# Stick-breaking attention scored three units ahead, with its running sums multiplied as two reduced-precision parts

## The reference

```
z = q k^T * scale                                   # masked: key < query
log_1m_beta = log_sigmoid(-z)                       # = -softplus(z)
between = reverse_cumsum(log_1m_beta) - log_1m_beta # over the keys
out = exp(log_sigmoid(z) + between) v
```

## Time and profile before

| | |
|---|---|
| median of 3 runs | 1580.63 us (1580.37 to 1584.75) |
| profiled execution, its own time | 1585.6 us |
| its span in the trace | 1583.5 us |
| mean granted TensorE clock | 0.977 of full |
| busy, share of the span | PE 94%, DVE 42%, ACT 33%, POOL 19% |
| the stage `heads` with its attention units | from 530.8 us to about 762.8 us |

### The profile page before, as it was taken

How to read it: one execution, slowest core, us unless ns; L and a number is a source line. 1 busy time by engine, 2 the same in 40 slices (tenths; PEclk the granted TensorE clock), 3 DMA queues, 4 the chain that set the end, 5 groups by cost and what they waited for, 6 DMA issues and landing times.

```text
span 1583.5 us, 27315 instructions
## 1 busy us (share of the span) xinstructions
PE 1481.2 (94%) x11281; PEld 1144.9 (72%) x11281; DVE 663.1 (42%) x1053; ACT 525.4 (33%) x945; POOL 306.2 (19%) x412
## 2 busy tenths in 40 slices
PE   5989989989898898998999999999999999999997
PEld 5767777767677554554678788888888888888876
DVE  5244152555653353546274424233332424242336
ACT  4432231433322466767343402122030403021122
POOL 5574615423241241513000100000000000000000
PEclk9999989999999899999999999999999999999999
DMA  5544413423233603003242312112020202111015
GB/s 184 139 136 134 113 42 99 130 57 96 58 83 96 175 5 81 2 2 127 95 152 80 123 37 66 40 40 66 9 97 0 93 13 66 40 43 63 26 44 182
DMA packets 134937, 124.10 MB, mean 78 GB/s; under 512 B 20813, under 2 KB 112138, under 8 KB 134842
## 3 DMA queue, kind: packets, MB, share of 16 engines
q1 hardware_dynamic: 88556, 92.90, 18.9%
q10 hardware_dynamic: 46286, 29.84, 6.7%
HBM read 97.88 MB, written 24.84 MB: 77 GB/s over the span
## 4 chain that ended last, share of the span: by engine, by line
PE 46%; DVE 2%; ACT 1%; DMA 1%; issue 1%; POOLq 0%; SPq 0%; DVEq 0%; ACTq 0%
PE all_ps_b L2028 22%; PE all_ps_b L2005 21%; PE all_ps_b L1577 2%; DMA bk_acc<-in_w_out 1%; POOLq L1597 0%; DVE bk_acc L1872 0%; PE all_ps_b L1998 0%; ACT bk_acc L1766 0%; DVE bk_acc L1882 0%; DVE bk_w1L L1843 0%; DVE bk_acc L1868 0%; DVE all_hL L1888 0%; DVE all_gL L1914 0%; ACT bk_rect L1797 0%; DVE bk_acc L1955 0%
## 5 line engine op out<-in xcount | busy, mean ns | idle before, releaser
L2005 PE MATMUL all_ps_b<-all_hH,bk_w1L 128*128 128x512 f32 x512 | 200.2, 391 | 5.4 <-PE all_ps_b L2028 2.1
L1924 DVE TENSOR_TENSOR bk_acc<-bk_acc,all_ps_b 128x512 f32<-128x512 f32 x128 | 88.0, 688 | 276.0 <-PE all_ps_b L2028 275.2
L2028 PE MATMUL all_ps_b<-bk_w2H,all_gL 128*128 128x512 f32 x512 | 199.9, 390 | 2.5 <-DVE all_gL L1914 2.5
L2028 PE MATMUL all_ps_b<-bk_w2L,all_gH 128*128 128x512 f32 x512 | 199.9, 390 | 0.0
L2028 PE MATMUL all_ps_b<-bk_w2H,all_gH 128*128 128x512 f32 x512 | 199.7, 390 | 0.0
L2005 PE MATMUL all_ps_b<-all_hH,bk_w1H 128*128 128x512 f32 x512 | 199.3, 389 | 0.0
L2005 PE MATMUL all_ps_b<-all_hL,bk_w1H 128*128 128x512 f32 x512 | 199.2, 389 | 0.0
L1205 PE MATMUL fr_ps_F<-fr_hH,fr_wL 128*128 128x512 f32 (+1 forms) x416 | 175.0, 421 | 7.2 <-POOL fr_wL L457 7.2
L457 POOL TENSOR_TENSOR fr_wL<-fr_raw,fr_wH 128x256 fp32r<-128x256 f32 (+1 forms) x208 | 162.1, 811 | 32.6 <-ACT fr_wH L502 29.3
L1205 PE MATMUL fr_ps_F<-fr_hH,fr_wH 128*128 128x512 f32 (+1 forms) x416 | 165.2, 397 | 0.0
L1205 PE MATMUL fr_ps_F<-fr_hL,fr_wH 128*128 128x512 f32 (+1 forms) x416 | 165.0, 397 | 0.0
(11 more groups left out here) (343 smaller groups left out, 2238.2 us busy)
## 6 DMA issues: line engine op xcount, KB each, us to landing
fr_raw<-in_w_in ACTq DMA_DIRECT2D x37, 512.0 KB, 4.2
bk_raw<-in_w_ff SPq DMA_DIRECT2D x32, 512.0 KB, 4.2
all_raw<-in_w_ff SPq DMA_DIRECT2D x32, 512.0 KB, 4.8
projected<-fr_stage ACTq DMA_DIRECT2D x39, 256.0 KB, 4.4
fr_raw<-in_w_in SPq DMA_DIRECT2D x13, 512.0 KB, 4.3
fr_xt<-in_x SPq DMA_DIRECT2D x8, 512.0 KB, 5.5
bk_acc<-in_x SPq DMA_DIRECT2D x8, 512.0 KB, 3.3
x_after_mixers<-bk_acc SPq DMA_DIRECT2D x8, 512.0 KB, 2.7
```

The lines of the kernel that those rows point to most:

```text
L1924: dve.tensor_tensor(acc[:, j, ds], acc[:, j, ds], ybank[g % 4][:], ALU.add).then_inc(collected, 1)
L2005: m = pe.matmul(bank[s][h][:], w[s][:, k, :], a[:, k, hs], start=(k == 0 and q == 0), stop=(k == KB - 1 and q == 2))
L2028: m = pe.matmul(ybank[g % 4][:], a[:, i, ts], w[:, i, ds], start=(i == 0 and q == 0), stop=(i == FB - 1 and q == 2))
```

## The change

1. AHEAD goes from 2 to 3. On PE the order within a unit becomes sums(u), scores(u+3), values; on ACT weight(u), then exp and ln of unit u+3 next to each other (a new `logs`). PE issues the first three scores of the next pair at the end of a pair, and ACT their logs.
2. The softplus is written over E (SP = E). The wait for POOL's running sum moves from DVE's softplus to ACT's exponential.
3. POOL copies the softplus to an fp32r tile SPH (`high`), DVE subtracts it one unit later into SPL (`low`), and `sums` multiplies fp32r `tri` by both instead of float32 `tri` by SP. The matmul of `ones` by R stays float32.
4. POOL's running sum and the GLA pieces of POOL and DVE move one unit behind in their queues. DVE's `scale`, the copies of the mixed result and SPLIT_AT move later (SCALE_AT 7 to 8, SPLIT_AT 8 to 10). Two of DVE's 13 `split_low` come after the last unit.

```diff
-    NZ, AHEAD = 4, 2
+    NZ, AHEAD = 4, 3
-        SP = [r.sb(f"SP{n}", [P, HALF]) for n in range(4)]
+        SP = E
+        SPH = [r.sb(f"SPH{n}", [P, HALF], F32R) for n in range(4)]
+        SPL = [r.sb(f"SPL{n}", [P, HALF], F32R) for n in range(3)]
-        SQUARE_AT, SUM_AT, ROOT_AT, SCALE_AT = 0, (2, 4), (3, 5), 7
-        HIGH_AT, LOW_AT = SCALE_AT + 2, SCALE_AT + 4
-        SPLIT_AT = 8
+        SQUARE_AT, SUM_AT, ROOT_AT, SCALE_AT = 0, (2, 4), (3, 5), 8
+        HIGH_AT, LOW_AT = SCALE_AT + 1, SCALE_AT + 4
+        SPLIT_AT = 10
 # POOL
+                def high(u):
+                    pool.wait_ge(s("sp"), i * NU + u + 1)
+                    if u >= 4 or i:
+                        pool.wait_ge(s("tri_mm"), i * NU + u - 3)
+                    pool.tensor_copy(SPH[u % 4][:, span(u)], SP[u % 4][:, span(u)]).then_inc(s("sp_high"), 1)
+                for u in range(NU):
+                    high(u)
+                    if u:
+                        running(u - 1)
+                    gla(i * NU + u - 1)
+                running(NU - 1)
 # ACT
+            def logs(i, u):
+                act.wait_ge(s("z"), i * NU + u + 1)
+                if u >= 4 or i:
+                    act.wait_ge(s("sum"), i * NU + u - 3)
+                act.activation(E[u % 4][:, span(u)], Z[u % NZ][:, span(u)], ACT.Exp).then_inc(s("exp"), 1)
+                act.wait_ge(s("exp"), i * NU + u + 1)
+                act.activation(E[u % 4][:, span(u)], E[u % 4][:, span(u)], ACT.Ln, bias=1.0).then_inc(s("log"), 1)
 # DVE
+                def low(u):
+                    dve.wait_ge(s("sp_high"), i * NU + u + 1)
+                    if u >= 3 or i:
+                        dve.wait_ge(s("tri_mm"), i * NU + u - 2)
+                    dve.tensor_tensor(SPL[u % 3][:, span(u)], SP[u % 4][:, span(u)],
+                                      SPH[u % 4][:, span(u)].bitcast(F32), ALU.subtract).then_inc(s("sp_low"), 1)
                 for u in range(NU):
                     softplus(u)
+                    if u:
+                        low(u - 1)
...
-                    gla(i * NU + u)
+                    gla(i * NU + u - 1)
+                low(NU - 1)
+            for n in range(NU - AHEAD - SPLIT_AT, len(ahead.pieces)):
+                ahead.split_low(dve, n)
 # PE
-                    pe.wait_ge(s("sp"), i * NU + u + 1)
-                    m = pe.matmul(z, tri[:], SP[u % 4][:, span(u)], start=False, stop=True, skip_group_check=True)
+                    pe.wait_ge(s("sp_high"), i * NU + u + 1)
+                    pe.matmul(z, tri[:], SPH[u % 4][:, span(u)], start=False, stop=True, skip_group_check=True)
+                    pe.wait_ge(s("sp_low"), i * NU + u + 1)
+                    m = pe.matmul(z, tri[:], SPL[u % 3][:, span(u)], start=False, stop=True, skip_group_check=True)
```

More of the change, by code:

```diff
@@ L2613, in units, with running @@
                 nth = [0, 0]
-                for u in range(NU):
+                def high(u):
[3 more added lines that the diff above has]
+                    pool.tensor_copy(SPH[u % 4][:, span(u)], SP[u % 4][:, span(u)]).then_inc(s("sp_high"), 1)
+                def running(u):
                     h, c, kb, off, first = UNITS[u]
@@ L2674, in mixed_high, with take_values @@
                 act.copy(ahead.hH[:, i, :], outT[:]).then_inc(s("m_high"), 1)
-            def units(i):
[L2677 to L2691, removed]
+            def take_values(i, n):
+                act.wait_ge(s("v_mm"), i * 2 + n + 1)
+                act.copy(vn[:, 4 * n:4 * n + 4, :], X[:].rearrange("p (j f) -> p j f", f=P)).then_inc(s("v"), 1)
+            def logs(i, u):
[5 more added lines that the diff above has]
+                act.activation(E[u % 4][:, span(u)], E[u % 4][:, span(u)], ACT.Ln, bias=1.0).then_inc(s("log"), 1)
+            def units(i):
                 def weight(u):
@@ L2697, in weight @@
                     act.activation(W[u % 4][:, span(u)], Z[u % NZ][:, span(u)], ACT.Exp).then_inc(s("weight"), 1)
-                for u in range(-AHEAD, NU):
+                for u in range(NU):
+                    weight(u)
                     if u + AHEAD < NU:
[L2701 to L2705, removed]
-                    elif i < LAST:
-                        split(i + 1, u + AHEAD - NU)
+                        logs(i, u + AHEAD)
+                    elif i < LAST:
+                        if u < NU - 1:
+                            split(i + 1, u + AHEAD - NU)
+                        else:
+                            for n in range(AHEAD):
+                                logs(i + 1, n)
                     if i == LAST and 0 <= u - SPLIT_AT < len(ahead.pieces):
@@ L2710, in units @@
                     if u == 0:
-                        take_values(1)
+                        take_values(i, 1)
                     if u == TAKE_AT:
@@ L2721, in units @@
                         mixed_high(i - 1)
-                    if u >= 0:
-                        gla(i * NU + u)
+                    gla(i * NU + u)
                 take_output(i, 1)
+                if i < LAST:
+                    take_values(i + 1, 0)
             act.preload_act_table_set(EXP_LN)
             act.wait_ge(s("eps"), 1)
+            take_values(0, 0)
+            for n in range(AHEAD):
+                logs(0, n)
             for i in range(PAIRS):
@@ L2873, in values @@
                     m.then_inc(s("v_mul"), 1)
-                for u in range(-AHEAD, NU + 1):
+                for u in range(NU + 1):
+                    if u < NU:
+                        sums(u)
                     if u + AHEAD < NU:
-                        scores(u + AHEAD)
-                    if 0 <= u < NU:
-                        sums(u)
+                        scores(i, u + AHEAD)
+                    if u == NU - 1 and i < LAST:
+                        for n in range(AHEAD):
+                            scores(i + 1, n)
                     if u >= 2 and u % 2 == 0:
                         values(u - 2)
+                    if u == NU and i < LAST:
+                        turn_values(i + 1, 0)
                     if u == 0:
@@ L2885, in units @@
                         squares(i - 1, SUM_AT.index(u))
-                    if 0 <= u < NU:
+                    if u < NU:
                         gla(i * NU + u)
+            turn_values(0, 0)
+            for n in range(AHEAD):
+                scores(0, n)
             for i in range(PAIRS):
```

37 lines of the change are left out of this document (16 added, 21 removed).

## The result

| | median us | runs |
|---|---|---|
| before | 1580.75 | 13 |
| changed kernel | 1586.64 | 13 |

The ratio is 1.0029 (95% interval 1.0017 to 1.0041): slower by 0.3%, where 1575.0 was forecast.

What follows compares the result with a forecast made beforehand. The stage was taken as PE-bound in 86 us and bound by chains across engines in most of the rest. -4.2 + 1.6 - 2.8 - 0.8 + 0.6 = -5.6 us took 1580.63 to 1575.0; range 1561 to 1588.

Steps and rivals of the forecast that it cites:

- Ends of pairs 0 and 1, -4.2: Units 14 to 23 of pairs 0 and 1: PE's saving partly lost, -2.1 us each, bounds 0 and -7.2.
- Load permits it: Ends of pairs 0 and 1: DVE at 21.7 and 24.0 us, POOL about 17, fit within 28.3 and 27.3.
- The chain: Ends of pairs 0 and 1: sums(u-2) through softplus and subtraction to `ones`, 4.3 us plus about 0.2 for two units.
- Narrow units, -0.8: Units 0 to 13 of pairs 0 and 1, 0 to 7 of the last: together -0.8 us, bounds -7 and +8.
- The comparison behind a wait: Narrow units, way to the next weight: a wash at 512 columns, a loss of 0.1 to 0.3 at 128 and 256.
- The +3.5 for ACT's exponential behind the weight: Narrow units: ACT reaches its linear-attention piece one exponential later, some six places at 0.6, +3.5 us.
- The last pair, +1.6: Last pair: subtractions and POOL's work exclude each other, 2.72 us a unit against 2.58; +1.6 us, bounds -3.6 and +6.
- Steps, -2.8: Between pairs, last weight to first: splits one unit earlier, scores ahead; -1.4 us twice, bounds 0 and -5.
- Start, +0.6: Before the first sums: one more unit's scores and logs and one subtraction, +0.6 us.
- PE's saving: Triangular sums: two fp32r matmuls for one float32 save 0.40 us a unit at 512 columns; ceiling 21.5 us.
- the slower one: Rival: VectorE and GpSimd exclude each other on every unit's path, `low` behind POOL's addition; about 1590 us, chance 0.22.
- The chain rival: Rival: `low` behind every linear-attention wait; ends of pairs 0 and 1 give 0, boundaries half; 1580.6 us, chance 0.25.

Runs made afterwards that it cites:

- the order alone: Changed kernel without the two-part sum: new order kept, one float32 triangular matmul of the softplus, no copy or subtraction; 1569.03 us, 0.9919 of the kernel before.
- no wait of PE: Changed kernel, but PE's second half multiplies the rounded copy again and awaits no remainder, which DVE still makes; 1578.29 us, 0.9971 of the kernel before.
- the later pieces: Kernel before with only DVE's and POOL's linear-attention pieces moved one unit later; 1579.36 us, 0.9974 of the kernel before.
- with the pieces back in place: New order without the two-part sum, with DVE's and POOL's linear-attention pieces back in their own unit; 1583.12 us, 1.0008 of the kernel before.
- Reading PSUM: Changed kernel, DVE's subtraction reading scores in PSUM times zero instead of the softplus, PE waiting for it before both halves; 1586.99 us, 1.0019 of the kernel before.
- the work: Changed kernel with every remainder made but none awaited by PE (1578.29 us), against the changed kernel without DVE's subtraction and its waits (1562.65): 15.6 us.
- the control of the PSUM run: Changed kernel with its own subtraction, but PE waits for it before both halves of the triangular sum; 1587.47 us, 1.0039 of the kernel before.
- the remainder in its own turn: Changed kernel with DVE making each unit's remainder at the end of that unit's turn, behind the linear-attention piece; 1594.22 us, 1.0069 of the kernel before.

## Why the prediction was wrong

- **Ends of pairs 0 and 1, -4.2.** This is the first step that failed: +0.2 and +2.2, so +2.4. "DVE comes to 21.7 and 24.0 us [...] Load permits it": DVE came to 27.0 and 29.3. Two terms were missing. The order brings more into these windows before any subtraction is made (17.4 and 19.4 in the order alone against 14.9 and 17.2): in pair 0 the second of the next pair's two splits, 2.45 us of DVE, in pair 1 part of that and one more piece of the linear attention. The forecast had the splits "issued one unit earlier", but counted them in the step alone. And the meetings with POOL stretch rows of DVE, which the forecast counted in the last pair only, on the ground that low, copy and addition, 2.2, lie below 3.0: the nine subtractions by 0.15 and 0.17 each (0.83 and 0.85 for 0.68), and the linear-attention rows of two inputs by some 2.3 us in pair 0 (2.14 for 1.23 above, and two others with 2.20 for 0.84). With this load and no wait of PE the ends took 30.2 and 31.6, where 28.4 and 27.8 were to be had; with the wait they took 32.1 and 33.1. The chain was right to be named (4.3 us for two units); what it left out is `low` standing behind a piece that waits.
- **Narrow units, -0.8.** +5.4, inside the bound of +8, and 6.2 us off the forecast where the ends are 6.6 off. By the forecast's own sign ("if the narrow units change by over 5 us either way") this is wrong too. The comparison behind a wait was made from softplus on ("0.69 + 0.68 + 0.23 + 0.86"). It missed that the later pieces take the softplus out from behind the piece (-6.4 measured for them alone, -6.0 with the whole order) and that `low` puts PE's operand back (+11.4 on top). The +3.5 for ACT's exponential behind the weight is not refuted: with the pieces back in place these units were 3.1 longer than before. No run has that reordering of ACT alone.
- **The last pair, +1.6.** Right: 39.2 to 40.6 us, +1.4, with the period 2.72 that was summed from the earlier trace rows. Without the split it is 38.5.
- **Steps, -2.8.** -1.3 (12.7 to 11.4). The order alone does more, -4.1; in the changed kernel the second step lost it.
- **Start, +0.6.** +0.5. **PE's saving.** 0.40 a unit was right where nothing else bound: 0.39 and 0.34 in two ends (3.5 and 3.1 us in nine steps).
- Of the rivals, the slower one (1590, chance 0.22) came nearest in time, but not by its own mechanism, `low` behind POOL's addition in every unit. Reading PSUM takes that away and the median stays. The chain rival (1580.6, chance 0.25) named the wait that was found, "`low` behind every linear-attention wait", with ends of pairs 0 and 1 that give nothing, and placed it in the ends, where it costs less than in the narrow units. What both lacked was DVE's own load. The sum of the terms above is +8.3 before rounding, and so is the stage's own change from the first scores to the last values (230.0 to 238.3 us, one execution of each); the medians say +5 to +6.

What stays open: how the 15.6 us of the work divide between DVE's own 0.68 and the exclusion in pairs 0 and 1. An instruction of 0.68 us that neither PE awaits nor POOL meets was not tried, since reading the bank without PE's wait would leave the two unordered. Why pair 1's step varies from 4.5 to 9.5 us among these kernels is not settled either. It goes with the granted clock: in every run whose step took 5.8 us or less the clock there was 1.00, and in every one of 6.4 or more it was 0.64 to 0.87 (0.77 in the change, 0.87 before). PE's idle time ahead of it does not decide that by itself: PE stood idle for 2.44 us before the new scores in the change and for 2.52 in the control of the PSUM run, where the clock stayed at 1.00. So part of what the table gives to a step is the clock of that one execution.

## What to carry to other kernels

Before moving work from a full engine to one at half load, write out the receiving engine's queue and ask what the full engine's next operand will stand behind: an instruction that waits for a third engine can cost nearly its whole wait there (3.45 of 3.81 us in the round shown). Test each part alone: here a change of order worth 0.8% was hidden under an addition that cost more. And count the receiver's load in the window where the donor is full, after all that the change moves into it, with the durations it has while its neighbour works.

## What the runs showed of the hardware

- A `tensor_scalar` from SBUF (float32) to SBUF (fp32r) takes 0.43 us for 512 columns, where the two-input subtraction takes 0.68; beside a POOL addition of 1.27 it took 1.47, so its speed is lost when the two meet.
- A subtraction of 16 columns that PE must wait for cost 10.7 us over 72 units (within some 5), though its row is 0.16 us where nothing meets it and 0.29 on average. Its place in an in-order queue has a price of its own.
- Two engines that exclude each other fall into a fixed period (2.72 us in the change, 3.45 with the remainder in its own turn), and each then shows rows 0.2 to 1.1 us longer than alone. In the change the period is the sum of what each instruction adds from the end of the one before it (0.47, 0.55, 1.15, 0.55), each about 0.1 us below its lone duration where a row shows one (0.68 for 0.55, 1.27 for 1.15).
